# Eight modulation pieces: from matmuls on TensorE to multiply-and-add steps on VectorE

## What is computed

```
mod = silu(cond) @ w_ada + b_ada          # cond: 2 rows of 1024; w_ada: 1024 x 6144
sh1, sc1, g1, sh2, sc2, g2 = split(mod, 6)
h = rmsnorm(x, g_pre_mix) * (1 + sc1) + sh1
x = x + g1 * rmsnorm(token_mixer(h), g_post_mix)
h = rmsnorm(x, g_pre_ffn) * (1 + sc2) + sh2
x = x + g2 * rmsnorm(expert_choice_ffn(h), g_post_ffn)
```

## Time and profile before

| | us |
|---|---|
| median of three timed runs | 1711.43 (1710.7 to 1713.13) |
| span of the profiled execution, first to last instruction | 1708.6 |
| TensorE busy | 1529.9 (90%) |
| VectorE busy | 473.3 (28%) |
| ScalarE busy | 337.0 (20%) |
| GpSimd busy | 90.0 (5%) |

### The profile page before, as it was taken

How to read it: one execution, slowest core, us unless ns; L and a number is a source line. 1 busy time by engine, 2 the same in 40 slices (tenths; PEclk the granted TensorE clock), 3 DMA queues, 4 the chain that set the end, 5 groups by cost and what they waited for, 6 DMA issues and landing times.

```text
span 1708.6 us, 15782 instructions
## 1 busy us (share of the span) xinstructions
PE 1529.9 (90%) x6391; PEld 711.7 (42%) x6391; DVE 473.3 (28%) x1111; ACT 337.0 (20%) x873; POOL 90.0 (5%) x121
## 2 busy tenths in 40 slices
PE   6999999999999999999998897877888877978787
PEld 2655555565545555556433332222222222322233
DVE  3437878740015555433111110000010000101002
ACT  2336565510023332012000000000000000010101
POOL 0003222200000001000000000000000000000000
PEclk9999999999999999999999999999999999999999
DMA  8234343324321535548999999999999999999995
GB/s 358 99 113 173 124 168 129 105 81 187 133 97 64 214 132 199 219 195 370 405 430 431 433 431 430 432 431 432 433 429 430 431 430 434 431 432 430 431 429 248
DMA packets 29608, 512.42 MB, mean 300 GB/s; under 512 B 3505, under 2 KB 3889, under 8 KB 9825
## 3 DMA queue, kind: packets, MB, share of 16 engines
q1 hardware_dynamic: 23472, 490.67, 68.7%
q0 software_dynamic: 5920, 20.61, 3.6%
q10 hardware_dynamic: 144, 0.13, 0.0%
HBM read 506.59 MB, written 4.82 MB: 299 GB/s over the span
## 4 chain that ended last, share of the span: by engine, by line
PE 52%; DMA 34%; DVE 9%; ACT 3%; issue 2%; SPq 0%; DVEq 0%; ACTq 0%
DMA arena<-in_expert_chunks 33%; PE psum L1051 14%; PE psum L703 7%; PE psum L461 6%; PE psum L675 5%; PE psum L472 3%; PE psum L1022 2%; PE psum L750 2%; PE psum L852 2%; DMA arena<-in_mixer_chunks 1%; ACT arena L1504 1%; DVE arena L1920 1%; PE psum L1071 1%; PE psum L742 1%; PE psum L484 1%
## 5 line engine op out<-in xcount | busy, mean ns | idle before, releaser
L1051 PE MATMUL psum<-arena 128*64 128x512 f32 x1856 | 435.0, 624 | 85.5 <-DMA arena<-in_expert_chunks 85.5
L1051 PEld LDWEIGHTS psum<-arena 128*64 128x64 f32 x1856 | 139.8, 143 | 366.7 <-issue 293.9
L1071 PE MATMUL psum<-arena 128*64 128x512 f32 x896 | 203.5, 608 | 48.4 <-DMA arena<-in_expert_chunks 48.4
L461 PE MATMUL psum<-arena 128*128 128x384 f32 x512 | 169.0, 487 | 0.0
L2315 DVE TENSOR_TENSOR arena<-arena,psum 128x512 f32<-128x512 f32 x30 | 20.6, 688 | 434.1 <-PE psum L1051 412.2
L1071 PEld LDWEIGHTS psum<-arena 128*64 128x64 f32 x896 | 63.8, 139 | 180.3 <-issue 116.1
L703 PE MATMUL psum<-arena 128*128 128x384 f32 x384 | 127.9, 486 | 0.0
L472 PE MATMUL psum<-arena 128*128 128x512 f32 x288 | 126.3, 594 | 0.0
L461 PEld LDWEIGHTS psum<-arena 128*128 128x128 f32 x512 | 96.2, 190 | 65.9 <-issue 3.4
L1657 ACT ACTIVATE arena<-psum 32x512 f32<-32x512 f32 (+1 forms) x70 | 38.2, 546 | 422.7 <-PE psum L1071 391.0
L1677 ACT ACTIVATE arena<-psum 128x512 f32<-128x512 f32 x30 | 17.9, 597 | 395.6 <-PE psum L1051 370.1
(11 more groups left out here) (282 smaller groups left out, 1277.2 us busy)
## 6 DMA issues: line engine op xcount, KB each, us to landing
arena<-in_expert_chunks SPq DMA_DIRECT2D x82, 4096.0 KB, 22.0
arena<-in_mixer_chunks SPq DMA_DIRECT2D x40, 2048.0 KB, 7.9
arena<-in_expert_chunks SPq DMA_DIRECT2D x24, 2048.0 KB, 13.1
arena<-cs_rows POOLq DMA_DIRECT2D x24, 512.0 KB, 5.0
arena<-in_expert_chunks SPq DMA_DIRECT2D x6, 1024.0 KB, 18.3
arena<-in_h_cm POOLq DMA_DIRECT2D x8, 256.0 KB, 3.0
out_state<-arena POOLq DMA_DIRECT2D x8, 256.0 KB, 2.6
arena<-in_x_cm SPq DMA_DIRECT2D x1, 1536.0 KB, 6.7
```

The costliest lines, as they stand in the source:

```text
L461: mm = pe.matmul(b[:, 0:NTOK], w[:, k, ct * P:(ct + 1) * P], src[:, k, :], start=k == 0, stop=k == KT - 1)
L1051: mm = pe.matmul(psum[HALF * q:HALF * (q + 1), hidden_banks(e, u)[up], :], x_in[:, k, :], w[q][:, k, :], start=k == 0, stop=k == KT - 1, t ...
L1071: mm = pe.matmul(psum[HALF * q:HALF * (q + 1), 5 + e % 2, :], hT[:, KT * u + k, :], w[q][:, k, :], start=bool(not u and k == 0), stop=bool ...
```

## The change

Pieces 4 to 11 leave TensorE's `ada`. VectorE multiplies each of the eight k-blocks of a piece by a per-partition scalar (`cond[:, k, c]`) and adds them, once for each of the two conditions: 16 steps of 128 x 512 for a piece, 128 in all (`ada_steps`), the sums staying in the weight buffer. TensorE adds up the partitions of two pieces at a time (`ada_summed`: four matmuls with 32 columns of ones), VectorE copies that (`ada_row`), TensorE turns it (`ada_turned`: four transposes), and VectorE adds the bias into `mod` (`ada_out`).

The loads of the pieces move forward: 4 and 5 behind `x` 5, and 6 to 11 between `o_ssd` 2 and `o_ssd` 3, into slots 2, 3 and others. `v` 0 takes slot 2 and `v` 1 takes slot 3 after pieces 6 and 7, whose end of use is `ada_turned(6)`. The steps stand in VectorE's order beside the B/C items (32) and beside and behind the merges of `o_ssd` (96). The attention steps lose their modulation fills, and so does the stretch before the experts. The halved `o_ssd` tiles lie in `ssd_proj`. The first expert's banks are swapped in pairs, and one early expert load moves ahead.

```diff
-    todo += [w_in("v", 0, 2), w_in("v", 1, 3), w_in("q", 0, 0), w_in("k", 0, 1), w_in("ga", 0, 2), ada(4), ada(5)]
-    todo += [w_in("q", 1, 0), ada(6), w_in("k", 1, 1), ada(7), w_in("ga", 1, 2), ada(8), ada(9)]
-    todo += [(("o_attn", 0), "w_o_attn", 0, 0, 0), ada(10)]
+    todo += [*ring[:2], ada(4, "d"), ada(5, "e"), *ring[2:-1]]
+    todo += [ada(6, 2), ada(7, 3), ada(8, "b"), ada(9, "f"), ada(10, "a"), ada(11, "g"), ring[-1]]
+    todo += [w_in("v", 0, 2), w_in("v", 1, 3), w_in("q", 0, 0), w_in("k", 0, 1), w_in("ga", 0, 2)]
+    todo += [w_in("q", 1, 0), w_in("k", 1, 1), w_in("ga", 1, 2), (("o_attn", 0), "w_o_attn", 0, 0, 0)]
...
-            if 1 <= h <= 5:
-                ending[3 * h] = ("ada", 3 + h)
-        middle[NA - 3], middle[NA - 2], middle[NA - 1] = ("ada", 9), ("ga", 7), ("ada", 10)
+        middle[NA - 2] = ("ga", 7)
...
+            def ada_summed(n):
+
+                pe.wait_ge(sem("ada_step"), 16 * (n - 2))
+                b = x_bank()
+                for q in range(4):
+                    mm = pe.matmul(b[32 * q:32 * q + 32, :], ones[:, 0:32], ada_sums(n + q // 2)[:, q % 2, :],
+                                   start=True, stop=True, tile_position=(0, 32 * q))
+                x_done(mm)
+                summed_at[n] = n_x[0]
+
+            def ada_turned(n):
+
+                pe.wait_ge(sem("x_free"), summed_at[n])
+                b = x_bank()
+                for ct in range(4):
+                    mm = pe.transpose(b[:, ct * P:(ct + 1) * P], ada_rows(n)[:, ct * P:(ct + 1) * P], ident)
+                x_done(mm)
+                for m in (n, n + 1):
+                    chunk_used(("ada", m), "x_ready", n_x[0])
...
             for ct in range(4):
                 cm_tile(("x", 0), ct)
+                if ct == 1:
+                    ada_summed(4)
+            ada_turned(4)
...
+                    if j and k2 == 0:
+                        ada_summed(6)
+            ada_turned(6)
+            ada_summed(8)
...
-            x_ring_is(5, 3)
             AT["v0"] = n_p[0]
             for t in range(NT):
                 tm_tile(("v", 0), t)
+                if t == 0:
+                    ada_turned(8)
+            ada_summed(10)
             for t in range(NT):
                 tm_tile(("v", 1), t)
+                if t == 0:
+                    ada_turned(10)
+                    x_ring_is(5, 3)
...
-            pe.wait_ge(sem("yg_ready"), 3)
-            p_done(ada(11, p_bank()))
-            chunk_used(("ada", 11))
...
-            for n in range(NM - 1):
+            for n in range(NM):
                 slot, m = chunk_slot[n], last_in_slot[n]
-                if slot in (2, 3) and m is None:
+                if n == chunk_no["ada", 5]:
+                    used("ada", 2)
+                if n == chunk_no["ada", 6]:
                     sp.wait_ge(sem("ssd_over"), 1)
...
+                    else:
+                        so_far = w[:, 0, :] if c_ == 0 else ada_part
+                        dve.wait_ge(sem("ada_step"), i - 1)
+                        dve.scalar_tensor_tensor(w[:, 1, :] if (k, c_) == (KT - 1, 1) else so_far, w[:, k, :], by, so_far,
+                                                 ALU.mult, ALU.add).then_inc(sem("ada_step"), 1)
...
+                    if it and it[0] == "x" and it[1] >= 4:
+                        ada_steps(4)
+                    if it == ("x", 0, 2):
+                        ada_row(4)
...
             items([("x", 0, c_) for c_ in range(4)])
+            ada_out(4)
...
             for i in range(KT):
+                if i == 4:
+                    ada_steps(18)
+                    ada_row(6)
+                    ada_steps(4)
                 dve.wait_ge(sem("p_free"), AT["gs"] + i + 1)
...
+                ada_steps((7, 7, 7, 11, 7, 7, 6, 0)[i])
+            ada_out(6)
+            ada_steps(6)
+            ada_row(8)
+            ada_steps(6)
+            ada_out(8)
+            ada_steps(10)
+            ada_row(10)
+            ada_out(10)
```

More of the change, by code:

```diff
@@ L342, in build, with ada_sums, ada_rows @@
         NA = len(pairs)
-        middle, ending = {}, {}
+        middle = {}
         for h in range(A_HEADS - 1):
             middle[3 * h], middle[3 * h + 1], middle[3 * h + 2] = ("q", h + 1), ("k", h + 1), ("ga", h)
-            if 1 <= h <= 5:
-                ending[3 * h] = ("ada", 3 + h)
-        middle[NA - 3], middle[NA - 2], middle[NA - 1] = ("ada", 9), ("ga", 7), ("ada", 10)
-        def modulations(i):
-            return [work[i][1] for work in (middle, ending) if i in work and work[i][0] == "ada"]
+        middle[NA - 2] = ("ga", 7)
+        def ada_sums(n):
+            return weight_slot[chunk_slot[chunk_no["ada", n]]][:, 0:2, :]
+        def ada_rows(n):
+            return weight_slot[chunk_slot[chunk_no["ada", n]]][:, 2, :]
         TILES = (1, 2, 0)
@@ L492, in ada_cm @@
                 for ct in range(4):
-                    row = late_row if j == 11 else mod_rows[:, j % 2]
-                    mm = pe.transpose(b[:, ct * P:(ct + 1) * P], row[:, ct * P:(ct + 1) * P], ident)
+                    mm = pe.transpose(b[:, ct * P:(ct + 1) * P], mod_rows[:, j % 2, ct * P:(ct + 1) * P], ident)
                 x_done(mm)
                 AT["ada_x"].append(n_x[0])
+            def ada_summed(n):
[14 more added lines that the diff above has]
+                    chunk_used(("ada", m), "x_ready", n_x[0])
+            summed_at = {}
             def first_ada(n):
@@ L694, in fill @@
                 b = psum[:, 4]
[L695 to L707, removed]
+                key = (kind, n // 4)
+                w = chunk(*key)
+                for k in range(KT):
+                    mm = pe.matmul(b[:, 0:NTOK], w[:, k, n % 4 * P:(n % 4 + 1) * P], h1T[:, k, :],
+                                   start=k == 0, stop=k == KT - 1)
+                mm.then_inc(sem("f_ready"), 1)
+                if n % 4 == 3:
+                    chunk_used(key, "f_ready", n_f[0])
                 if kind in ("q", "k"):
@@ L791, in _ @@
                     o_at.append(n_x[0])
[L792 to L795, removed]
             def spread(n):
@@ L1550, in filled @@
                     return
[L1551 to L1556, removed]
+                act.activation(gaT[:, n, :], b[:, 0:NTOK], ACT.Tanh, scale=0.5).then_inc(sem("f_free"), 1)
             act.wait_ge(sem("merged_ready"), KT)
@@ L1761, in ada_cm, with ada_steps, ada_row, ada_out @@
                 link(dve.tensor_tensor(m4, m4, wide(vec_a[:, 4 * j:4 * j + 4], 2), ALU.add))
+            ada_ops = [(n, k, c_) for n in range(4, 12) for k in range(KT) for c_ in (1, 0)]
+            ada_done = [0]
+            def ada_steps(count):
+                for i in range(ada_done[0], ada_done[0] + count):
+                    n, k, c_ = ada_ops[i]
+                    slot = chunk_slot[chunk_no["ada", n]]
+                    w, by = weight_slot[slot], cond[:, k, c_:c_ + 1]
+                    if (k, c_) == (0, 1):
+                        dve.wait_ge(sem(f"w_in_slot{slot}"), 16 * (slot_load[chunk_no["ada", n]] + 1))
+                    if k == 0:
+                        if i:
+                            dve.wait_ge(sem("ada_step"), i)
+                        dve.tensor_scalar(w[:, 0, :] if c_ == 0 else ada_part, w[:, 0, :], by, None, ALU.mult)\
+                           .then_inc(sem("ada_step"), 1)
+                    else:
[3 more added lines that the diff above has]
+                                                 ALU.mult, ALU.add).then_inc(sem("ada_step"), 1)
+                ada_done[0] += count
+            def ada_row(n):
+                b = x_take()
+                x_free(dve.tensor_copy(ada_rows(n), b[:, :]))
+            def ada_out(n):
+                b = x_take()
+                parts = b[:, :].rearrange("p (a q r) -> p a q r", a=4, q=4)
+                for m in (n, n + 1):
+                    j, q = ADA_ORDER[m], 2 * (m - n)
+                    last = dve.tensor_tensor(mod[:, 4 * j:4 * j + 4, :], parts[:, :, q:q + 2, 0],
+                                             wide(vec_a[:, 4 * j:4 * j + 4], 2), ALU.add)
+                x_free(last)
             def affine(dst, sc, sh, gain, lo=0, n=KT):
@@ L2214, in _ @@
             logits(0)
-            ada_cm(11)
             affinity(0)
```

35 lines of the change are left out of this document (13 added, 22 removed).

## The result

The changed kernel takes 1720.45 us (median of 4 runs, 1720.01 to 1722.68) against 1711.59 us (median of 4) for the kernel before: ratio 1.0055, 95% interval 1.0044 to 1.0067. The forecast was 1717.6, slower, with a range of 1711 to 1722. The profiled execution of the changed kernel spans 1720.9 us against 1708.6, so the two traces to be compared differ by 12.3 us, some 3 us more than the medians do. It is the slowest of the four (1722.68, so that 1.8 us lie outside its span, and not the 3 told of the kernel before). At least 1.7 of the 12.3 us belong to the execution and not to the change, as will be seen.

The account below looks back on a forecast made before the run. After 800 us transfers bound the kernel; before, mostly TensorE, so its lateness at the first expert counts: 2.0 + 1.5 + 8.0 + 1.8 + 3.0 − 10.1 = +6.2 us on 1711.4, forecast 1717.6, range 1711 to 1722.

Parts of the forecast that it names:

- three signs: Wrong if TensorE idles under 5 us before `v` 0, attention shortens over 12 us, or `o_ssd`'s second half waits.
- The wait for `v` 0: After `o_ssd`: the load can be issued only after `ada_turned(6)`, so TensorE waits, +8.0 us (7.2 to 8.5).
- The half clock behind it: Work after the wait for `v` 0 runs at clock 0.50, one loss of +1.8 us (0 to 2.5).
- The attention: Attention steps without pieces: five pieces give 1.91 us each, −9.55; pieces 9 and 10 give 0.
- Rival (b): Faster: all TensorE work of eight removed pieces counts, 19.8 us, so −3.5 in total, 1707.9; chance 0.1.
- `o_ssd`: Loads and VectorE steps beside `o_ssd` stay hidden; sums +0.93 and `ada_turned(6)` +0.6 bring lateness to +3.5.
- rival (c): Slower still: `o_ssd` 3 lands 3 us late amid `o_ssd`, with a second clock fall; +11.0, 1722.4; chance 0.12.
- VectorE's steps: Each 128 x 512 step on VectorE takes 0.66 us, between 0.62 and 0.69.
- Part 4: Value projection: turns, sums, a 0.35 us wait for the last ten steps and the ring switch, +3.0 (2.0 to 4.5).
- Part 1: B/C items to scan: sums, additions and cumulative sums behind `ada_out(4)` make TensorE +2.0 us late (+0.9 to +3.2).
- Part 5: What the removed pieces give back, attention to experts: −10.1 us (−9.5 to −15.8), with 0 for piece 11.
- rival (a): A tie: clock doesn't fall or falls inside the wait, scan 0.9 late, value part 2.0; +1.8, 1713.2; chance 0.2.

Follow-up runs that it names:

- the repeat: The changed kernel, unaltered, measured once more beside the first group of experiments: 1723.08 us, ratio 1.0069 to the kernel before.
- e1: Changed kernel with the transposes of pieces 6 and 7 moved up into the second half of `o_ssd`: 1713.08 us, ratio 1.0011.
- e2: Kernel before, with only the load of `v` 0 held back until TensorE has finished `o_ssd`: 1722.38 us, ratio 1.0066.
- e5: Changed kernel with VectorE's steps 8 columns wide in place of 512, same order and semaphores: 1722.14 us, ratio 1.0062.
- e7: Changed kernel with pieces 6, 7 turned early, 4, 5 late, and unread matmuls filling waits before the scan and in the routing: 1707.53 us, ratio 0.9980.
- e8: Kernel before with unread fill matmuls, eight ahead of the scan and twice three in the routing: 1709.86 us, ratio 0.9989.
- e3: Changed kernel with eight unread matmuls put where piece 11 had stood: 1720.07 us, ratio 1.0057.
- e10: e7 without its fills, against the changed kernel only the early and late turning: 1711.5 us, ratio 0.9996.
- e9: e7 with pieces 10 and 11 back on TensorE in their old places, 11 replacing its eight fills: 1705.5 us, ratio 0.9960.

## Why the prediction was right, and where it was off

The measured 1720.45 lies in the range; the repeat's median, 1723.08, lies 1 us above it. None of the three signs that the forecast named for being wrong came: TensorE's idle time before `v` 0 was 6.95 us, the attention got 9.5 shorter, and TensorE didn't wait in the second half of `o_ssd`. But the first expert, told for near 793.4, came at 798.53.

**The wait for `v` 0: right.** 8.0 said, 7.92 in the trace. e1 takes the release forward and the wait is gone; e2 puts it alone into the kernel before and the whole loss is there.

**The half clock behind it: right in kind, +2.16 for +1.8.** The sum took one piece's loss, 1.67 us; the value tile lost 2.16, and e2's four tiles 2.5. The Trainium skill's section named in the prediction (TensorE: Matmul & The Clock Gate, HAM oscillation) describes a wait for a transfer with a throttled TensorE behind it, and the trace agrees: 6.95 us of waiting, then a granted clock of 0.50.

**The attention: right in this execution.** −9.52 for −9.55. Steps 3 and 6 are 21.08 us apart (547.60 and 568.68 in the chain), the value of the stretch without a piece. Pieces 9 and 10 gave 0 and 0.23, and the output projection starts 0.41 nearer, for 0.5 said; that the total fits to 0.03 is in part luck, since the first steps came 0.27 later. Rival (b), with 2.47 us a piece in every place, falls with this: eight would have been 19.8, and 9.9 came. But the 0 for piece 9 left out the clock, like that for piece 11 below: where half clock follows the wait that it leaves (five of the eight executions with all eight pieces moved), the attention is 1.6 us longer, and the gain is 7.9.

**`o_ssd`: right.** +1.65 for +1.5. The sums of piece 6 cost 0.99 and its turn 0.46, and TensorE waited for nothing in the second half (20.91 and 20.84 us for its two passes of 64 records), so rival (c) did not occur.

**VectorE's steps: right, on the slow side.** 112 steps have a mean of 745 ns, more than the 692 of the product taken as nearest; back to back, ten come in 6.71, one each 0.67 us, where 0.66 was taken. By the Trainium skill's table (VectorE: DVE Perf Modes, perf-mode tier table), which has no row for this operation, the estimate from `tensor_tensor` was 0.57; the measurement decides, and it was 0.67. e5 shows that nothing hangs on it.

```profile
478.23 13.90 PE L476 MATMUL psum<-arena 128*128 128x512 f32 x32
478.58 6.71 DVE L1798 SCALAR_TENSOR_TENSOR arena<-arena 128x512 f32<-128x512 f32 x10
492.06 1.07 PE L506 MATMUL psum<-arena 128*32 128x512 f32 x8
...
500.95 5.43 PE L730 MATMUL psum<-arena 128*128 128x384 f32 x16 [0.33 <-DVE arena L1813]
```

**The value part, Part 4: mis-sized, +2.40 for +3.0.** The step that failed is "7.2 in all against two tiles of 6.9". One value tile takes 6.87 us, two of them 13.90 (first line), so ten steps (second line) are over long before piece 10's sums are asked for at 492.06, and the 0.35 of waiting are not there. It was a misreading of a row: 64 records in 27.63 us are four tiles, so one takes 6.9. The ring's wait is 0.33, for 0.6.

**Up to the scan, Part 1: mis-sized, +3.67 for +2.0, beyond its upper bound of 3.2.** The mechanism was as told: the cumulative sums, which had run ahead of the wait, now stand behind `ada_out(4)`. But the terms missed the clock. After 2.88 us of idle time it was at half for 6.8 us (107.5 to 114.4), where the kernel before had 3.4 (106.1 to 109.6): one more spell, 1.7 us, and 3.67 − 1.7 = 2.0. How many spells come varies with the execution: one in e5, none in e2 with the code of the kernel before. With the clock at 1.00 and the output late the pieces cost 1.6 (e7 less e8).

```profile
108.00:110.00 2.00, 2.00 (x12) 2.00 (x11) 1.11 (x2) 0.00 (x0) 0.00 (x0) 0.50 0.81 344
112.00:114.00 2.00, 2.00 (x10) 1.44 (x9) 0.87 (x2) 0.00 (x0) 0.00 (x0) 0.50 0.00 0
```

**Piece 11, Part 5: 0 said, +1.84 measured in the routing.** "Piece 11 ran while VectorE searched the best tokens ... 0" is right for the work and says nothing of the clock: its eight matmuls had also kept TensorE busy in a stretch full of short waits. Half clock held for 3.4 us there before and for 10.2 after, and for 10.2 in each of the six executions without work in that place. How much of the 1.84 is due to the missing piece is not settled: filling its place alone (e3) shortened the stretch by a third only, and the kernel before, in e2's execution, had 6.8 us of half clock there too. What is shown is that with the waits at the scan and in the routing filled the clock stays up in both, and about 2.7 us come back (e10 against e7).

**The remainder.** +1.66 in the first projection belongs to the execution. So does the +0.93 in the expert part, as far as the traces tell: from the first expert's matmuls to the end, the twelve executions take 921.0 to 924.1 us, and the two kernels e2 and e8, with the pieces where they were before, have the shortest and the longest. So the sum of +6.2 was right in its main mechanism, the late release, and low by two to three half-clock spells, to which the prediction gave a price only behind the large wait: the changed kernel's medians lie 9 and 12 us above the kernel before's. The tie, rival (a), needed the clock not to fall behind the wait; it did fall.

## What to carry to other kernels

When work moves to an idle engine and keeps its buffer longer, look for the instruction that releases that buffer and for what is loaded into it next: here arithmetic of 76 us was free, and one release behind a stage instead of in the middle of it cost 9 to 10 us. A matmul that only fills a wait has a value of its own when the engine's clock falls in waits, so "hidden" work should be priced twice, by its time and by the clock of what follows. Only pieces that stood on the critical path should be moved; those in waits are best left (e9 for pieces 10 and 11; piece 9 was in such a place too).

## What the runs showed of the hardware that was not expected

- Short waits were followed by a granted clock of 0.50 in place of 1.00: 1.78 us in the attention, 1.86, 2.40 and 2.88 at the scan. The stretches at 0.50 were some 3.4, 6.8 or 10.2 us long. Each 3.4 us of solid matmul work at half clock cost 1.7 (the first projection, 43.24 in place of 41.55).
- The same wait does not always do it: the 1.78 us in the attention did in six executions of nine. At the scan, 2.40 us of idle time were followed by half clock in the kernel before, and 2.41 us in e2, with the same instructions, were not. In e2's timeline:

```profile
106.52 0.59 PE L568 MATMUL psum<-arena 128*128 128x192 f32 x2 [2.41 <-DVE arena L1857]
```

- Executions of the same code therefore differ by whole spells: 41.55 or 43.24 us in the first projection, whichever kernel ran. A difference of 1.7 us between two single traces is no finding here.
- Eight matmuls with a 32-column target (sixteen records) took 1.92 us on four places of the array, and fitted into the 2.40 us wait at the scan, of which 0.56 was left (e7).
